# RWKV-7 layer of a four-layer encoder: loop and output stage in one block, pair products in 64x64 blocks, key norms two at a time

## The reference

```python
def rwkv7_mixer(h, w_in, mu, w0, w2, a0, a2, k_k, k_a, r_k, ln_g, ln_b, w_out):
    proj = h @ w_in + dx @ (w_in * mu_cols)
    r, k, v, g, w_lo, a_lo = _split(proj, RW_WIDTHS)
    ...                                        # decay and a from w_lo and a_lo
    kk = k * k_k
    kk = kk / jnp.maximum(jnp.sqrt(jnp.sum(kk * kk, axis=-1, keepdims=True)), 1e-12)
    k = k * (1.0 + (a - 1.0) * k_a)
    b_vec = kk * a
    def step(S, inp):                          # 16 heads of 64 x 64
        sa = jnp.einsum('bhvk,bhk->bhv', S, -kk_t)
        S = S * w_t + sa[..., None] * b_t + v_t[..., None] * k_t
        return S, jnp.einsum('bhvk,bhk->bhv', S, r_t)
    _, y = lax.scan(step, S0, xs)
    y = head_norm(y, ln_g, ln_b, RW_GN_EPS)
    y = y + jnp.sum(r * k * r_k, axis=-1, keepdims=True) * v
    return (y * jax.nn.silu(g)) @ w_out
```

## Time and profile before

| | |
|---|---|
| median of 3 runs | 1463.33 us (1460.79 to 1463.57) |
| the profiled execution | 1463.39 us, of which its span is 1461.6 us |
| PE busy | 1366.8 us (94% of the span) |
| DVE busy | 723.2 us (49%) |
| ACT busy | 398.5 us (27%) |
| POOL busy | 96.0 us (7%) |
| mean granted TensorE clock | 0.977 |

### The profile page before, as it was taken

How to read it: one execution, slowest core, us unless ns; L and a number is a source line. 1 busy time by engine, 2 the same in 40 slices (tenths; PEclk the granted TensorE clock), 3 DMA queues, 4 the chain that set the end, 5 groups by cost and what they waited for, 6 DMA issues and landing times. The chain is left out here.

```text
span 1461.6 us, 21217 instructions
## 1 busy us (share of the span) xinstructions
PE 1366.8 (94%) x9011; PEld 721.3 (49%) x9011; DVE 723.2 (49%) x1404; ACT 398.5 (27%) x900; POOL 96.0 (7%) x114
## 2 busy tenths in 40 slices
PE   5999999999798999879899989998999999999887
PEld 3444455489544444564434436544444455479633
DVE  5784664966643002261345023434684763966552
ACT  1114355044201011460122053501113256134401
POOL 0000242001000000000000000000000143011000
PEclk9999999999999999999999989999999999999999
DMA  6221222100500222101222221122322222200221
GB/s 209 72 72 50 67 58 58 44 3 4 217 17 0 76 83 72 58 2 58 73 60 85 72 58 29 44 72 74 120 58 72 58 59 58 58 2 4 74 118 58
DMA packets 111174, 92.29 MB, mean 63 GB/s; under 512 B 5020, under 2 KB 99524, under 8 KB 110568
## 3 DMA queue, kind: packets, MB, share of 16 engines
q1 hardware_dynamic: 110376, 88.81, 20.0%
q10 hardware_dynamic: 704, 2.13, 0.4%
HBM read 84.64 MB, written 6.29 MB: 62 GB/s over the span
## 5 line engine op out<-in xcount | busy, mean ns | idle before, releaser
L888 PE MATMUL bank<-arena 128*128 128x512 f32 x960 | 423.7, 599 | 1.5 <-ACT arena L555 1.5
L888 PEld LDWEIGHTS bank<-arena 128*128 128x128 f32 x960 | 182.0, 191 | 227.3 <-issue 221.1
L843 PE MATMUL bank<-arena 64*64 64x64 f32 (+5 forms) x5440 | 195.3, 235 | 10.4 <-issue 4.5
L843 PEld LDWEIGHTS bank<-arena 64*64 64x64 f32 (+3 forms) x5440 | 171.0, 141 | 47.4 <-issue 38.3
L1204 PE MATMUL bank<-arena 128*128 128x512 f32 x256 | 116.5, 616 | 4.7 <-DVE arena L1168 4.7
L159 ACT ACTIVATE arena<-arena 128x1024 f32<-128x1024 f32 x20 | 21.1, 1055 | 243.2 <-DVE arena L1174 132.1
L1204 PEld LDWEIGHTS bank<-arena 128*128 128x128 f32 x256 | 50.0, 198 | 70.9 <-issue 64.5
L1668 PE MATMUL bank<-arena 128*128 128x512 f32 x160 | 71.1, 605 | 1.6 <-PEq L301 1.6
L653 DVE SCALAR_TENSOR_TENSOR arena<-arena 128x512 f32<-128x512 f32 x96 | 71.9, 798 | 0.0
L581 ACT ACTIVATE arena<-arena 32x128 f32<-32x128 f32 x128 | 54.0, 422 | 57.1 <-DVE arena L675 54.4
L505 POOL MEMSET arena<- 128x8 f32 x2 | 0.2, 112 | 933.0 <-DVE arena L805 933.0
(11 more groups left out here) (230 smaller groups left out, 1606.3 us busy)
## 6 DMA issues: line engine op xcount, KB each, us to landing
arena<-in_rw_w_in SPq DMA_DIRECT2D x66, 512.0 KB, 4.0
arena<-in_ml_w_in SPq DMA_DIRECT2D x24, 512.0 KB, 3.8
arena<-in_sw_w_in SPq DMA_DIRECT2D x20, 512.0 KB, 3.8
arena<-in_rw_w_out SPq DMA_DIRECT2D x16, 512.0 KB, 8.2
spill<-arena SPq DMA_DIRECT2D x2, 2048.0 KB, 9.4
arena<-spill SPq DMA_DIRECT2D x2, 2048.0 KB, 14.2
arena<-in_sw_w_out SPq DMA_DIRECT2D x8, 512.0 KB, 3.8
arena<-in_ml_w_out SPq DMA_DIRECT2D x8, 512.0 KB, 3.7
```

What stands on the lines that cost most here:

```text
L843: mm = lambda out, a, b, start=True, stop=True: nc.tensor.matmul(out, a, b, start=start, stop=stop, skip_group_check=True)
L888: last = nc.tensor.matmul(bank[:, :], slot[:, k, :], mix_at[what][:, k, :], start=k == 0, stop=k == KT - 1)
```

## The change

- `rw_mix` and `rw_gate_out` become one function and one block, `rw_layer`.
- `pair_products` writes each pair product as two matmuls with weights 64x64 in place of one with weights 64x128: 32 matmuls a call in place of 16. It serves `products_a` and `products_r`.
- The key norms run two at a time after every second key tile, the first two after k2, the last two after r0. Each pair is four matmuls 64x64 by 512 columns; the second tile of a pair leaves with its two heads' partitions exchanged, and ScalarE takes its root in two halves. VectorE handles norm j two key tiles later.
- The mixes of g are spread over chunks 0 to 3, two in each.
- In the last chunk the sums of squares of the first 7 chunks (`sums(0, ...)`) stand before `solve`, two bonus products before `outputs`; the state update of that chunk, its `turn_bk` and `keep_bkt`, and the VectorE `advance` are gone. The sums of the last chunk come after it, from a square that ScalarE takes directly. The reciprocal is split into 448 and 64 columns.
- Three of the eight bonus products are copied by ScalarE and multiplied by GpSimd, not by VectorE.
- The loads of `w_out` and `pick` are issued after the state update of chunk 6, the reload of h after the last `solve`. A square root on one element in chunk 2 loads ScalarE's table. The table of constants grows by 16 columns.

The pieces in the order of the diff: the list of tiles; the key norms on TensorE; the pair products; VectorE beside the values; the chunk loop on TensorE and what follows it; the sums; VectorE after the chunk loop.

```diff
-    tiles += [("k", j)] * (j < KT) + [("n2", j - 1)] * (j > 0)
-tiles += [("r", j) for j in range(EARLY_R)] + [("lora", 0)]
+    tiles += [("k", j) if j < KT else ("r", 0)] + [("n2", i) for i in range(j - 2, j) if j > 0 and j % 2 == 0]
+tiles += [("r", j) for j in range(1, EARLY_R)] + [("lora", 0)]
...
 elif what == "n2":
-    pe.wait_ge(kk_squared.handle, kk_squared.at(j + 1))
-    last = nc.tensor.matmul(bank[:, :], bones, sq[j % 2], start=True, stop=True)
+    if j % 2:
+        return
+    pe.wait_ge(act_done.handle, act_done.at(max(n - 6, 0)))
+    pe.wait_ge(kk_squared.handle, kk_squared.at(j + 2))
+    for rows, others in ((LO, HI), (HI, LO)):
+        ones = bones[rows, rows]
+        first = mm(bank[rows, :], ones, sq[0][rows])
+        last = mm(tile_bank(n + 1)[others, :], ones, sq[1][rows])
+    first.then_inc(tile_done.handle, 1)
...
 def pair_products(c, p, query, banks, inc):
-    for par, rows in SIDES:
-        last = mm(banks[par][:, C * p:C * p + C], both(p, c)[rows], query[rows, p, span(c)])
-        if p == KT - 1:
-            last.then_inc(inc.handle, 1)
+    for side, out in SIDES:
+        for par, rows in SIDES:
+            last = mm(banks[par][out, C * p:C * p + C], both(p, c)[rows, C * side:C * side + C], query[rows, p, span(c)])
+            if (p, side) == (KT - 1, 1):
+                last.then_inc(inc.handle, 1)
...
 for c in range(NC):
     if c + 1 < NC:
         scale(c + 1)
-    if c == 1:
-        mix("g")
     mask_a(c)
     if c + 1 < NC:
         scale_k(c + 1)
+    if c < BC:
+        mix("g", (2 * c, 2 * c + 1))
...
     if c + 1 < NC:
         turn_values(c + 1)
         x(c + 1)
+    else:
+        sums(0, 0, SUMMED)
     solve(c)
     state_outputs(c)
     if c + 1 < NC:
         products_r(c + 1)
+    else:
+        bonus(0)
+        bonus(1)
     outputs(c)
     if c + 1 < NC:
-        turn_bk(c + 1)
+        if c + 1 < NC - 1:
+            turn_bk(c + 1)
         xu(c + 1)
         right_side_values(c + 1)
+bonus(2)
+sums(1, SUMMED, T)
+for j in range(3, KT):
+    bonus(j)
 spread(range(4))
...
+def sums(n, at, to):
+    ...
+    for i in range(2):
+        for q in range(4):
+            last = mm(sums_bank[group(q, Q), at:to], compact(i), L[:, 4 * i + q, at:to], i == 0, i == 1)
+    last.then_inc(sums_done.handle, 1)
...
+invert_roots(0, 0, SUMMED)
+for j in range(3):
+    times_values(j)
+invert_roots(1, SUMMED, T)
+for j in range(3, BY_VALUES):
+    times_values(j)
+for j in range(KT):
+    finish(j)
```

More of the change, by code:

```diff
@@ L390, in heads, with rw_layer @@
     return buf.rearrange("p (k h) c -> p k h c", h=2)[:, :, par, :]
-def rw_mix(m, prm, w2a2, reset_src, n0, spill):
+def rw_layer(m, prm, w2a2, reset_src, n0, spill, w_out, pick_src, norm, final_g=None, out=None):
     nc = m.nc
@@ L487, in rw_mix @@
     links, steps = [0], [0]
+    W = m.view(B_K, KT, D)
+    pick = m.view(A_XT, D)
+    rstd = m.view(A_Z, T)
+    group = lambda j, n: slice(32 * (j % 4), 32 * (j % 4) + n)
+    compact = lambda i: m.view(A_CONST + C_COMPACT + 14 - 2 * i, Q)
+    fg = m.view(B_R, D)
+    eps = m.view(A_SMALL + 90, 1)
+    sums_bank = m.bank[0]
+    spread_bank = lambda j: m.bank[(4, 5, 0, 6)[j % 4]]
+    bonus_bank = lambda j: m.bank[(1, 2, 3, 6, 7)[j % 5]]
+    out_bank = lambda a, half: m.bank[RW_OUT_BANKS[half][a]]
+    eps_set, y_squared, last_squared, sums_done, root, inverse, pick_loaded, reloaded = (m.sem(n) for n in (
+        "eps_set", "y_squared", "last_y_squared", "sums_done", "root_ready", "rstd_ready", "pick_loaded", "h_reloaded"))
+    bonus_done, bonus_used, bonus_kept, bonus_times_v, spread_done, spread_used, finished, out_done = (m.sem(n) for n in (
+        "bonus_done", "bonus_used", "bonus_kept", "bonus_times_v", "spread_done", "spread_used", "y_finished", "out_done"))
+    w_loaded = [m.sem(f"w_out{k}_loaded") for k in range(KT)]
+    added, fg_loaded, stored = m.sem("h_added"), m.sem("final_g_loaded"), m.sem("stored")
     with nc.Block() as block:
@@ L496, in _ @@
             m.load_weights(sp, n0 + 33)
+            sp.wait_ge(s_done.handle, s_done.at(2 * NC - 2))
+            for q in range(4):
+                sp.dma_start(pick[group(q, 4), :], pick_src[4 * q:4 * q + 4, :]).then_inc(pick_loaded.handle, 16)
+            for k in range(KT):
+                sp.dma_start(W[:, k, :], w_out[k * P:(k + 1) * P, :]).then_inc(w_loaded[k].handle, 16)
+            sp.wait_ge(h_spilled.handle, h_spilled.at(16))
             sp.wait_ge(sa_done.handle, sa_done.at(NC))
+            sp.dma_start(m.view(A_H, 4096), spill[0]).then_inc(reloaded.handle, 16)
             m.load_weights(sp, n0 + 33 + SLOTS)
-            sp.wait_ge(h_spilled.handle, h_spilled.at(16))
+            if out is not None:
+                sp.wait_ge(bonus_done.handle, bonus_done.at(KT))
+                sp.dma_start(fg, final_g.unsqueeze(0).to_broadcast([P, D])).then_inc(fg_loaded.handle, 16)
+                for a in range(NT):
+                    sp.wait_ge(norm.scaled.handle, norm.scaled.at(a + 1))
+                    sp.dma_start(out[0, a * P:(a + 1) * P, :], norm.h[:, a, :]).then_inc(stored.handle, 16)
+                sp.wait_ge(stored.handle, 16 * NT)
         @block.gpsimd
@@ L611, in read_sa, with take_root, read_last_y @@
                     last.then_inc(sa_evac.handle, 1)
+            def take_root(n, at, to):
+                act.wait_ge(sums_done.handle, sums_done.at(n + 1))
+                nc.scalar.activation(rstd[:, at:to], sums_bank[:, at:to], ACT.Sqrt, bias=eps, scale=1.0 / C).then_inc(root.handle, 1)
+            def read_last_y():
+                for g in range(2):
+                    act.wait_ge(y_done.handle, y_done.at(2 * (NC - 1) + g + 1))
+                    nc.scalar.activation(L[:, pairs[g], span(NC - 1)], quarter(m.bank[4 + g]), ACT.Square)\
+                        .then_inc(last_squared.handle, 1)
+                for g in range(2):
+                    nc.scalar.activation(KK[:, pairs[g], span(NC - 1)], quarter(m.bank[4 + g]), ACT.Copy)\
+                        .then_inc(y_evac.handle, 1)
             def read_y(c):
@@ L768, in _ @@
             link(nc.vector.tensor_scalar(omka, m.view(prm + RW_KA, 8), -1.0, 1.0, ALU.mult, ALU.add))
-            for j in range(KT + 1):
+            for j in range(KT + 2):
                 if j < KT:
@@ new lines, in _, with add @@
+            invert_roots(0, 0, SUMMED)
[6 more added lines that the diff above has]
+                finish(j)
+            def add(dve, n):
+                dve.wait_ge(out_done.handle, out_done.at(n + 1))
+                part = norm.h[:, n % NT, 512 * (n // NT):512 * (n // NT) + 512]
+                nc.vector.tensor_tensor(part, part, out_bank(n % NT, n // NT)[:, :], ALU.add).then_inc(added.handle, 1)
@@ L841, in _ @@
+            dve.wait_ge(reloaded.handle, reloaded.at(16))
+            for a in range(NT):
+                add(dve, a)
+            if out is None:
+                nc.vector.memset(norm.xt[:, :, 0:1], 0.0)
+                norm.dve_steps(dve, lambda dve, a: add(dve, NT + a))
+            else:
+                dve.wait_ge(fg_loaded.handle, fg_loaded.at(16))
+                norm.dve_steps(dve, lambda dve, a: add(dve, NT + a), fg)
         @block.tensor
```

244 lines of the change are left out of this document (104 added, 140 removed).

## The result

The changed kernel takes 1421.52 us (median of 4 runs, 1420.37 to 1421.91); the kernel before, on the same chip, 1462.24 (4 runs). The ratio is 0.9717 [0.9705, 0.9729], so 41 us went. Forecast were 1405 us in a range of 1398 to 1424, a gain of 58. The direction and the range hold; a third of the gain is missing.

A forecast was written before the change was run, and what follows sets the result against it. TensorE, busy 94% of the span, was taken as the bound. A layer saves 16.6 (pair products, mixes) + 4.7 (keys) + 1.0 (last transposes) + 6.8 (end) = 29.1 us; two layers 58, 1463.4 - 58 = 1405 us, range 1398 to 1424.

The forecast's parts named there:

- Pair products, the price: Calls of pair products on TensorE: 64 small records take 0.98 us instead of 1.93, 0.95 us less a call.
- The rival with a fixed price for each matmul: Pair products: at 30 ns a record a call takes 1.9 us, no gain, 1434 us; chance 0.08 (1424 to 1440).
- Chunk loop: `products_r(1)` to `(7)` on TensorE stand in a full queue, so each split call counts: 7 x 0.95 = 6.65 us a layer.
- the transposes and `xu(0)`: Chunk loop: dropping `turn_bk(7)` saves 1.0 us a layer; `products_r(0)`, limited by the wait of `xu(0)` for `mask_r(0)`, 0.34.
- Values: Stage of `products_a`: eight shorter calls bring 7.6 us and a wait removed by spreading the mixes 1.98, a layer.
- The spread mixes: Values: mixes of g, two to a chunk, lie in VectorE's wait for the exponentials; TensorE's wait of 1.98 us goes.
- Keys: First key tile to `lora`: paired norms bring TensorE there 5.8 us sooner, less a wait of 1.1: 4.7 us a layer.
- the serial rival: Key norms: pairs run one after the other, 1.72 us each, bringing 2.4 instead of 4.7 us, 1410; inside the forecast's 0.66.
- The wait before `lora`: Before `lora`, TensorE waits 1.1 us for VectorE's mixes, 29.4 us against TensorE's 28.3 from the end of k7.
- The end: From `read_rhs(7)` to the first output product: 21.9 us becomes 15.1, so 6.8 us a layer.
- GpSimd beside VectorE: The end: GpSimd's last multiplication runs beside VectorE's first finish; 0.3 us was added for it.
- another engine becomes the bound: ScalarE's chain in the chunks or VectorE's at the keys has a missed latency, 12 us: 1417 (1412 to 1424); chance 0.16.

The follow-up runs named there:

- e2: The changed kernel with `products_a` alone back in 64x128 weights, `products_r` left in 64x64: 1435.19 us, ratio 0.9814.
- e1: The changed kernel with `products_r` alone back in 64x128 weights, `products_a` left in 64x64: 1421.77 us, ratio 0.9718.
- e3: The changed kernel with twelve more runs of the 64x64 products of chunk 0 ahead of `products_r(0)` in each layer: 1461.55 us, one run.
- e4: The changed kernel with twelve more runs of chunk 0's products, in 64x128 blocks, ahead of `products_r(0)` in each layer: 1464.51 us, one run.
- e6: The changed kernel with the key norms one at a time in their old places: 1428.96 us, ratio 0.9769.
- e5: The changed kernel with 4 of the 8 pairs of each `products_r` in 64x128 blocks, the other 4 in 64x64: 1418.83 us, ratio 0.9698.

## Why the prediction was right in sign and short in size

**Pair products, the price.** Nearly right: 1.09 us from the call to the next tile (forecast 0.98), so a call is 0.84 us shorter instead of 0.95, also by e2. The rival with a fixed price for each matmul falls for the record; yet a price of that size, 29 ns for a matmul, does exist where they follow each other for more than two blocks. The prediction read 30 ns from `state_outputs` and 16 from `solve` and chose between them as if one had to be the price. Both were short stretches, and no stretch of 32 records can show a supply that comes in blocks of 256 instructions.

**Chunk loop: the step that failed.** "`products_r(1)` to `(7)` stand in a full queue: 7 x 0.95 = 6.65 us." By e1 these splits are worth nothing. The queue was not full in the sense that mattered: the step looked at who releases an instruction and not at whether it has arrived. With the transposes and `xu(0)` the part was to bring 8.0 us and brought 1.2. The issue gaps named in the trace hold 4.08 of the missing 6.8; most of the rest is lost at the same place of a block, in shorter steps (under e3 and e4). The profile of before had hints, 71 transfers of instructions and a gap of 0.28 us put down to "issue" in the same loop; the rate at which blocks arrive was first measured in e3.

**Values.** 9.6 forecast, 10.4 measured in layer 3, a near hit of two misses. The eight calls bring 8 x 0.84 = 6.7 us instead of 7.6. The spread mixes bring 3.7 instead of 1.98, because with the wait goes the stretch of lower clock behind it (1188.48 to 1199.12 is 10.6 us where a chunk takes 9.0), and the prediction took the clock as it was. The two terms also depend on each other, since the stage before had two limits at once: TensorE at 9.0 us a chunk and a lump of 8.05 us on VectorE. The "1.98 us goes" of the sum is the wait behind wide products; behind small ones it is 3.63.

**Keys.** 4.7 forecast, 3.7 measured (e6: 7.4 us in two layers). A pair does not run serially: 1.02 us from its first record to the next tile (1023.86 to 1024.88), against 0.86 taken and 1.72 by the serial rival. The wait before `lora` is 1.04 us, as forecast (1.1). The rest of the miss stands at the entry to the pair: the key tile ahead takes 6.96 us (1016.90 to 1023.86) instead of 6.86. Four pairs at some 1.1 us instead of 0.86 are the missing 1.0 us. The Trainium skill, "TensorEngine Tiling (Array Packing)", Restrictions and Gotchas, says that different row tiles can't access the same PSUM bank simultaneously; the pair writes each bank from both row halves and isn't slowed to two passes, so the trace disagrees.

**The end.** 6.8 forecast, 5.8 measured. `spread` starts 11.97 us after `read_rhs(7)` (1335.68 to 1347.65) instead of 11.3; part of this is that the sums of 64 columns load for 0.66 us where 0.4 was taken. GpSimd beside VectorE costs 0.57 instead of 0.3.

**The rivals.** In size the result lies in "another engine becomes the bound" (1412 to 1424), but its mechanism is absent: no wait for ScalarE or VectorE appeared in the loop behind its first chunk. The right rival, TensorE's instruction supply, was not on the list. The range held because a rival of that size was there for another reason.

## What to carry to other kernels

Splitting matmuls into smaller tiles that run side by side buys time only until the engine's instructions arrive more slowly than they run; count the instructions of a loop, take 13.5 to 15 ns for each of TensorE's (this kernel's values), and compare with the time that the loop's own work would take after the split. Where the work comes out shorter, split only as many as balance the two, and expect single stalls even then (periods of 9.94 to 10.78 us in e5). Where two engines both limit a stage, the worth of relieving one depends on the other, so test the edits alone as well as together.

## What the hardware showed that was not expected

TensorE's instructions arrive as blocks of 256, in a long stream one in 3.45 us (layer 0) or 3.75 us (layer 3), so a stream of 64x64 matmuls by 64 columns runs for 2.09 us and stands for 1.36 or 1.65. The stalls show themselves by their place: always the same instruction of a block, 193 or 194 by this count. With 64x128 weights and 64 columns, a matmul takes 60 ns (1.93 us for 32), nearly four times a 64x64 one (16 ns). Where the form changes, the next call starts some 0.1 us later than the records alone account for (a call of 64 takes 1.09 us and not 0.98, the key tile ahead of a pair 6.96 and not 6.86); no run tests that by itself.
